# Merging two stages of the odd layer, splitting the feed forward's first weights one stage earlier, and normalising on GpSimd at the end of the first feed forward

## What is computed

```python
def channel_mixer(x, w1, w2):
    return jnp.square(jax.nn.relu(x @ w1)) @ w2
...
xp = layer_norm(DN_ALPHA * xp + mp, ln_mix_g[layer], ln_mix_b[layer])
xp = layer_norm(DN_ALPHA * xp + channel_mixer(xp, ffn_w1[layer], ffn_w2[layer]), ln_ffn_g[layer], ln_ffn_b[layer])
...
lse = jax.nn.logsumexp(s, axis=-1)
p = jnp.exp(s - lse[..., None])
...
wts = jax.nn.softmax(jnp.stack(lses), axis=0)
```

## Time and profile before

| | us |
|---|---|
| median of three runs | 4165.85 |
| the profiled execution | 4164.2 |
| its span (first to last instruction) | 4162.4 |
| TensorE busy | 3673.1 (88%) |
| VectorE busy | 1813.2 (44%) |
| ScalarE busy | 1081.7 (26%) |
| GpSimd busy | 648.1 (16%) |

### The profile page before, as it was taken

The page is one execution under the profiler, slowest core; times in us unless marked ns, Lnnn a source line. Parts: engine busy times, 40 slices in busy tenths (PEclk is TensorE's granted clock), DMA queues, the critical chain, the costliest instruction groups (busy, mean ns, idle before and its releaser), DMA issues. The chain is left out here.

```text
span 4162.4 us, 65277 instructions
## 1 busy us (share of the span) xinstructions
PE 3673.1 (88%) x25389; PEld 2934.3 (70%) x25389; DVE 1813.2 (44%) x2752; ACT 1081.7 (26%) x2297; POOL 648.1 (16%) x611
## 2 busy tenths in 40 slices
PE   7988888888679899999998999578875989999997
PEld 7965666666457798889985676256564479998886
DVE  2158433333585434444342344544044643344445
ACT  2156344444512112111113223211122021121112
POOL 0047111111001111111110111046001111111112
PEclk9999999999889999999999999689987999999998
DMA  2210999999502111111102100058302211111111
GB/s 94 74 46 1 354 408 405 405 405 403 183 25 92 31 41 40 40 50 40 50 30 87 44 26 19 11 189 290 101 22 73 75 41 51 40 40 40 45 46 64
DMA packets 220225, 470.66 MB, mean 113 GB/s; under 512 B 31609, under 2 KB 128741, under 8 KB 216886
## 3 DMA queue, kind: packets, MB, share of 16 engines
q1 hardware_dynamic: 199014, 446.49, 29.3%
q10 hardware_dynamic: 20976, 20.97, 1.6%
HBM read 447.50 MB, written 19.91 MB: 112 GB/s over the span
## 5 line engine op out<-in xcount | busy, mean ns | idle before, releaser
L1744 PE MATMUL f_u<-xH,f_w1h 128*128 128x364 f32 (+1 forms) x1536 | 508.3, 331 | 23.1 <-DVE f_w1l L1880 23.1
L1888 DVE TENSOR_TENSOR x<-x,f_d 128x512 f32<-128x512 f32 x576 | 392.1, 687 | 299.2 <-PE f_d L1744 281.2
L1744 PE MATMUL f_u<-xL,f_w1h 128*128 128x364 f32 (+1 forms) x1536 | 507.8, 331 | 0.0
L1744 PE MATMUL f_u<-xH,f_w1l 128*128 128x364 f32 (+1 forms) x1536 | 507.7, 331 | 0.0
L1744 PE MATMUL f_d<-f_w2h,f_hh 128*128 128x512 f32 x1024 | 408.4, 399 | 12.7 <-DVE f_w2l L1880 8.8
L1744 PE MATMUL f_d<-f_w2l,f_hh 128*128 128x512 f32 x1024 | 407.0, 397 | 0.0
L1744 PE MATMUL f_d<-f_w2h,f_hl 128*128 128x512 f32 x1024 | 406.8, 397 | 0.0
L1864 POOL TENSOR_TENSOR f_hl<-f_h,f_hh 128x364 fp32r<-128x364 f32 (+1 forms) x192 | 175.7, 922 | 1296.4 <-ACT f_hh L1830 1296.4
L822 DVE COPY ss_kT<-ss_tk 128x512 f32<-128x512 f32 x256 | 177.0, 692 | 392.3 <-PE ss_tk L714 242.2
L1905 DVE TENSOR_TENSOR f_h<-f_h 128x364 f32<-128x364 f32 (+1 forms) x192 | 103.1, 537 | 554.5 <-ACT f_h L1824 554.2
L1744 PEld LDWEIGHTS f_u<-xH,f_w1h 128*128 128x128 f32 x1536 | 291.6, 190 | 25.3 <-issue 12.3
(11 more groups left out here) (544 smaller groups left out, 6389.2 us busy)
## 6 DMA issues: line engine op xcount, KB each, us to landing
ss_kv<-in_cache_sb_kv SPq DMA_DIRECT2D x336, 512.0 KB, 8.1
x<-in_cache_sb_kv SPq DMA_DIRECT2D x176, 512.0 KB, 8.3
w<-in_ffn_w SPq DMA_DIRECT2D x64, 1024.0 KB, 5.2
mp_qb<-mp_q SPq DMA_DIRECT2D x24, 1024.0 KB, 7.2
x<-in_x_prompt SPq DMA_DIRECT2D x16, 512.0 KB, 7.8
pe_raw<-in_w_in_even SPq DMA_DIRECT2D x8, 1024.0 KB, 5.4
mp_kc<-in_cache_dil_kv SPq DMA_DIRECT2D x8, 1024.0 KB, 8.6
mp_vc<-in_cache_dil_kv ACTq DMA_DIRECT2D x8, 1024.0 KB, 6.4
```

Source lines behind the costliest of these rows:

```text
L1744: mm = pe.matmul(out, a, b, start=(n == 0), stop=(n == len(parts) - 1))
L1888: v.tensor_tensor(K.x[0:r, t, cs], K.x[0:r, t, cs], dn_b[(c * DOWN + u) % 4][0:r, :], ALU.add).then_inc(added, 1)
```

## The change

Four things are changed.

1. `FirstChunk` takes the place of `Ahead` for the feed forward's first chunk of w1, in both layers. It holds the high and low parts too. `project_and_norm` calls `set_high` on ScalarE after its tile step t = 5 and `set_low` on VectorE after t = 6. The feed forward's own copies of that chunk are replaced by a semaphore increment.
2. At the end of the first layer's feed forward GpSimd normalises tiles 0 to 6 with one `tensor_scalar` each. ScalarE keeps the normalisation of tiles 7 and 8. VectorE writes the second half of the turned columns of these two tiles. SyncE starts the load of `group_w` after the store of tile 6 is issued, once the first four tiles are stored and turned.
3. `dilated_prompt` for group 2 and `mlstm_rows` become one stage, `last_prompt_and_rows`. The tile loop has three buffers for `z` and one PSUM buffer for the scores. The matmuls of the gates stand behind the scores of tile 0 on TensorE. VectorE does the pieces of the rows between tiles (after steps 2, 4, 5, 6 and 7). `dilated_combine` follows it. The load of `mp_w` is issued behind the small loads, not ahead of them. The rows' buffers lie over `K.x`.
4. In `dilated_both` the rotary products `a_` and `b_` have one buffer, not two, so that VectorE's products of a tile wait for GpSimd's rotation of the tile before.

```diff
+                    if t == 6:
+                        ahead.set_low(v)
...
+                    if t == 5:
+                        ahead.set_high(a)
...
+        def wait_normed(eng, t):
+            if turn and t >= LATE:
+                eng.wait_ge(normed_late, t - LATE + 1)
+            else:
+                eng.wait_ge(normed, t + 1)
...
-                sp.wait_ge(stored, 16 * TT)
-                if turn:
-                    sp.wait_ge(turned, 2 * TT)
-                    ahead.start(sp)
+                    sp.dma_start(rows[t], K.x[0:rows_of(t), t, :]).then_inc(stored if t >= 4 else first_stored, 16)
+                    if turn and t == 6:
+                        sp.wait_ge(first_stored, 16 * 4)
+                        sp.wait_ge(turned, 2 * 4)
+                        ahead.start(sp)
...
-                high_w1(0, 0, 16)
+                a.sem_inc(w1_high, 1)
...
-                    for q in range(2):
+                    for q in range(2 if t < LATE else 1):
...
-                        a.wait_ge(shift_ready, t + 1)
+                        if not turn or t >= LATE:
+                            a.wait_ge(shift_ready, t + 1)
...
+                if turn:
+                    for t in range(LATE):
+                        g.wait_ge(shift_ready, t + 1)
+                        g.tensor_scalar(K.x[:, t, :], K.x[:, t, :], agg[:, t, 0:1], rstd[:, t:t + 1], ALU.subtract, ALU.mult).then_inc(normed, 1)
...
-                low_w(w1_high, w1l[0], w1h[0], w1_split, 0, 0)
+                v.sem_inc(w1_split, 1)
...
+                def keep_late(t):
+                    n = 2 * t + 1
+                    v.wait_ge(turned, n + 1)
+                    for f in range(4):
+                        k = 4 + f
+                        ins = v.tensor_scalar(turned_to(t, k), up_b[n % 4][:, f * P:f * P + rows_of(t)], gcol[:, 0, k:k + 1], gcol[:, 1, k:k + 1],
+                                              ALU.mult, ALU.add)
+                    ins.then_inc(late_kept, 1)
...
-        a_, b_, qk = sb("a", [P, 2, 2 * DW]), sb("b", [P, 2, 2 * DW]), sb("qk", [P, 2, 2 * DW])
+        a_, b_, qk = sb("a", [P, 2 * DW]), sb("b", [P, 2 * DW]), sb("qk", [P, 2, 2 * DW])
...
+                for t in range(NTL + 3):
+                    if t < NTL:
+                        scores(t)
+                    if t == 0:
+                        gates()
+                    if 2 <= t < NTL + 2:
+                        turn_weights(t - 2, 0)
+                    if t >= 3:
+                        values(t - 3)
+                    if 2 <= t < NTL + 2:
+                        turn_weights(t - 2, 1)
+                        turn_sums(t - 2)
+                turn_rows()
...
+                between = {2: forget, 4: decay, 5: maxima, 6: ends_of_chunks, 7: exponents_of_rows}
+                for t in range(NTL + 1):
+                    if t < NTL:
+                        centre(t)
+                    if t >= 1:
+                        scale(t - 1)
+                    if t in between:
+                        between[t]()
+                keep_columns()
...
+                    if t == 3:
+                        softplus()
+                    if t == NTL:
+                        row_exponents()
...
-            dilated_prompt(K, G, 2)
+            weights = Ahead(K, "mp_w0", [P, KD, MSLAB], io["w_in_odd"][0].rearrange("(k p) n -> p k n", p=P)[:, :, MC0 + MW:MC0 + MW + MSLAB])
+            last_prompt_and_rows(K, G, weights)
...
-            mlstm_rows(K, G, weights)
```

More of the change, by code:

```diff
@@ L1869, in _ @@
                 steps(body, None)(g)
-                if not turn:
+                if turn:
+                    for t in range(LATE):
+                        g.wait_ge(shift_ready, t + 1)
+                        g.tensor_scalar(K.x[:, t, :], K.x[:, t, :], agg[:, t, 0:1], rstd[:, t:t + 1], ALU.subtract, ALU.mult).then_inc(normed, 1)
+                else:
                     for t in range(TT):
@@ L1922, in last @@
                             scale_up(t - 1)
+                    if turn:
+                        v.wait_ge(gb_loaded, 32)
+                        for t in range(LATE, TT):
+                            keep_late(t)
                 def statistics(t):
@@ L3444, in program @@
         G["oTs"], G["lseTs"] = each("oTs", [P, 2, NSMP]), each("lseTs", [DILH, NSMP])
+        kept = ctx.enter_context(ExitStack())
+        G["Mrow"], G["cols"], G["wold"] = (kept.enter_context(nc.sbuf_tensor(n, shape, F32)) for n, shape in (
+            ("Mrow", [MH, NT]), ("cols", [P, TT, 4, MH]), ("wold", [P, MH, NE])))
+        G["Mrow_kept"] = nc.dram_tensor("Mrow_kept", (MH, SEQ), F32, kind="Internal").ap()
         with ExitStack() as dil:
@@ L3482, in program @@
             mlstm_sample(K, G)
+        kept.close()
         K.next_stage()
```

510 lines of the change are left out of this document (260 added, 250 removed).

## The result

The changed kernel takes 4137.98 us, the median of four runs (4137.29 to 4144.39), beside 4165.98 for the kernel before (4162.8 to 4171.89). The ratio is 0.9936, with a 95% interval of 0.9922 to 0.9949: faster by 28 us. In a second set of five runs it took 4135.72, with a ratio of 0.9923 (0.991 to 0.9937). The prediction was 4134, 4127 to 4147.

A forecast was written before the change was run, and what follows sets the result against it. TensorE was taken as the bound, busy 88% of 4162.4 us, so only its waits could move. Gains of 4.3 + 2.0 + 9.6 + 14.7 = 30.6 took 4164.2 to 4133.6; predicted 4134, range 4127 to 4147.

The forecast's parts named there:

- (c): End of the first feed forward: with GpSimd normalising and `group_w` loaded early, the next stage starts sooner; gain 9.6.
- (d): Merged stage of group 2's attention and the rows, T its start: ends at T+82.9; gain 14.7.
- (a): First w1 chunk, layer 0: its copy and subtraction move into the stage before, so TensorE starts earlier; gain 4.3.
- The cover: Layer 0: VectorE's wait of 2.69 for TensorE at tile 7 hides the moved subtraction; cost 2.3 if gone.
- (b): First w1 chunk, layer 1: 4.3 come off, but the subtraction puts 2.3 on VectorE's path; gain 2.0.
- hold: Merged stage: the softplus in ScalarE's step 3 holds up the logarithm VectorE wants next, about 1.9.
- (e): `dilated_both`: one buffer for `a_` and `b_` leaves GpSimd's rotation under the TensorE-bound step; cost 0.
- R1: Rival: the merged stage's step stays at 4.5 and its loads come at 8.1: 4143; chance 0.13.
- R3: Rival: TensorE's clock doesn't fall to half in the shorter gap, and layer 1 hides its subtraction: 4130; chance 0.10.
- R4: Rival: GpSimd's `tensor_scalar` is slow, c per tile; the kernel is slower than before only with c over 8.5; chance 0.02.
- R5: Rival: the gates or a queue delay the merged stage so that its gain is eaten: 4149; chance 0.04.
- R2: Rival: GpSimd beside VectorE slows both, stretching the tail's adds and statistics by 1.44: 4139; chance 0.06.

The follow-up runs named there:

- e7: Changed kernel, but in the second layer VectorE subtracts the first w1 chunk between its normalisation and bias addition of tile 7, in its wait for GpSimd: 4138.97 us.
- e5: Changed kernel, but SyncE starts the `group_w` load behind all stores and turns, as before; GpSimd still normalises: 4144.82 us.
- e10: Changed kernel, but GpSimd subtracts layer 1's w1 chunk, VectorE also writes tile 6's second half, and SyncE's wait for the last stores moves to the next stage: 4138.88 us.
- e11: Changed kernel with merged stage reordered, a shorter first feed-forward tail, and layer 1's low parts written in VectorE's wait for GpSimd: 4121.07 us.
- e1: The changed kernel, unaltered, run again: 4135.72 us, ratio 0.9923 to the kernel before.

## Why the prediction was right, point by point

The time was right, 4138 beside 4134, and inside the range. A part of this is luck: (c) fell 2.6 short, and C gained 1.8 more than (d) was forecast to. The size of each part, from the stretches of the table (C and D as means over all profiles of a kind):

- (a) predicted 4.3. A gives 4.2. The cover, the 2.69 of the earlier trace rows, held.
- (b) predicted 2.0. E costs 2.1, F gives 4.2: 2.1. That a step with a wait in its middle can't hide work placed elsewhere in its list was right. What the text missed is that the wait wouldn't have hidden it there either (e7): VectorE and GpSimd can't do two such operations side by side.
- (c) predicted 9.6, measured 7.0 (B, 48.6 to 41.6). The mechanism was right, and two terms were mis-sized. The first is "I take 2.4" for GpSimd's `tensor_scalar`. It took 3.77, outside the bounds of 1.24 and 2.44, both taken from other kinds of instruction on the grounds that they moved as many columns. It was held to be hidden and was not: one of the prediction's own signs of being wrong, the wait of the turns that names GpSimd, came. The first turn is 4.9 behind the first `f_agg`, not 3.7, with 1.00 of it that wait, and five steps of 3.77 in place of 3.67 add 0.5; so ScalarE ended 39.4 behind the first `f_agg`, not 37.5. The other term is the store: "some 3 us to land" was 6.1, behind the 2 MB of `group_w` in the same queue, and it ended the block 1.0 behind ScalarE (e5: without the load ahead of it, the 1.0 is gone). The prediction named what SyncE had left and costed it at nothing; in moving a load forward it did not ask what stands behind the load.
- (d) predicted 14.7. The first pair of profiles gives 14.8 (404.1 to 389.3), the means 16.5 (405.0 to 388.5), of which perhaps 2.8 are lost in `mlstm_project`. All terms held within 1.1 us: gates T+4.6 for 5.6, 16.8 long, step 3.65 for 3.62, hold 1.5 for 1.9, end T+81.8 for T+82.9. (The pieces of the rows, given as 2.9 and 15.0, stand in the sum as 17.6; by VectorE's rows they took 17.7.)
- (e) predicted 0. From `dilated_both`'s first projection to the stage behind it the first pair of profiles has 258.5 and 258.6. No run was made with this part alone undone.

Of the rivals, R1 didn't come: the step was 3.65 in spite of a clock of 0.61. R3: the clock's penalty stayed, and layer 1 hid nothing. R4: c was 3.77, above the bounds and far from the 8.5. R5 didn't come. R2 feared that GpSimd and VectorE slow each other, and was right in kind, but not for the tail, where VectorE's operations read one SBUF tensor. Its price, a stretch by 1.44, misreads the row it came from. The earlier trace rows leave out GpSimd's first product of that tile:

```profile
2482.17 0.73 POOL L2446 TENSOR_TENSOR db_qk<-db_a,db_b 128x256 f32<-128x256 f32 x1 [10.17 <-DVE db_b L2394]
```

VectorE's product (2482.22, 1.77) began 0.05 behind it and took 0.54 more than alone, which is nearly the rest of it. A product of half the size, in the same place of a later tile, takes 0.56 more (1.25 where it is 0.69 alone). So it is a wait for the other engine's operation, and not a slower pace; e7 and e10 show the same with longer ones.

## What to carry to other kernels

A price for an engine must come from the same instruction on the same engine; as many columns isn't enough (a product of two tensors took GpSimd 1.90 or 2.35, a `tensor_scalar` 3.77). Whoever moves a large load forward in a queue should ask what is issued behind it and who waits for that. And work can be hidden in a wait for GpSimd only if it doesn't need what GpSimd needs: the low parts, read from PSUM and one SBUF tensor, fitted (e11), the subtraction of two SBUF tensors didn't (e7).

## What the hardware showed beyond this

Between a VectorE operation with two SBUF inputs and one of GpSimd the lock was whole, and went by who started first, in every place looked at here: 0.16 ahead, VectorE kept GpSimd for 1.98; 0.08 ahead, GpSimd kept VectorE for 4.3; 0.05 ahead, it kept VectorE for 0.54 in the kernel before. What was left of the other's operation was 2.12, 4.45 and 0.68, each 0.14 or 0.15 more than the hold.

TensorE's clock at the start of `dilated_both` was a matter of the execution. Both rows are of the same program, behind the same idle time of 2.40, the changed kernel's first profile and its second (e1):

```profile
2319.38 8.95 PE L2214 MATMUL db_ps_q<-group_w,xT 128*128 128x512 f32 x16
```

```profile
2318.08 7.26 PE L2214 MATMUL db_ps_q<-group_w,xT 128*128 128x512 f32 x16
```

The granted clock of the first 10.4 us was 0.84 in the one and 1.00 in the other, so TensorE ran at 1.2 GHz for a while in the first, 1.7 us dearer. The second `dilated_both`, behind an idle time of 1.31 in both, began with the same two values. Together they are the 3.0 by which C fell. With `mlstm_project`'s 6 this is most of the scatter between executions, and the reason why parts of 2 us are read from stretches and not from medians.
